# Gate matrices by three bf16 products per token in place of one fp32 product

## What is computed

```
def peer_ffn(x, wq, keys, U, V):
    ...
    top_s, top_j = lax.top_k(cand, K)
    e1 = jnp.take_along_axis(i1, top_j // K, axis=-1)
    e2 = jnp.take_along_axis(i2, top_j % K, axis=-1)
    idx = e1 * N_KEYS + e2
    gate = jax.nn.softmax(top_s, axis=-1).astype(x.dtype)
    ...
        act = jax.nn.gelu(jnp.einsum('tkd,td->tk', U[it], xt), approximate=False) * gt
        return jnp.einsum('tk,tkd->td', act, V[it])
```

## Time and profile before

| what | value |
|---|---|
| median of 3 runs | 3653.57 us (3648.0 to 3656.35) |
| profiled execution, time | 3648.24 us |
| its span, first to last instruction | 3646.4 us |
| mean granted PE clock | 0.963 |
| PE busy / DVE / ACT | 94% / 54% / 33% of the span |
| chain that ended last | PE 87% of the span, of it L501 42%, L743 30%, L657 7%, L699 5% |

### The profile page before, as it was taken

The page is one execution under the profiler, slowest core; times in us unless marked ns, Lnnn a source line. Parts: engine busy times, 40 slices in busy tenths (PEclk is TensorE's granted clock), DMA queues, the critical chain, the costliest instruction groups (busy, mean ns, idle before and its releaser), DMA issues.

```text
span 3646.4 us, 47438 instructions
## 1 busy us (share of the span) xinstructions
PE 3426.9 (94%) x19384; PEld 2917.3 (80%) x19384; DVE 1979.2 (54%) x3330; ACT 1191.8 (33%) x1795; POOL 20.0 (1%) x41
## 2 busy tenths in 40 slices
PE   8899897999999999999999999798468999999998
PEld 7465546888888888888888888688458999999998
DVE  2204633488855555634444444333935998856665
ACT  1111224322233333333333333424314444444443
POOL 0000000000000000000000000000000000000000
PEclk9889898999999999999999999899789999999999
DMA  5241012355555556576556655222014777788885
GB/s 175 70 128 46 1 41 95 114 168 162 166 166 199 193 182 203 173 246 201 192 190 193 193 190 161 69 83 91 0 58 157 211 212 243 246 275 265 266 260 168
DMA packets 232862, 587.87 MB, mean 161 GB/s; under 512 B 21239, under 2 KB 104264, under 8 KB 229000
## 3 DMA queue, kind: packets, MB, share of 16 engines
q1 hardware_dynamic: 227536, 528.57, 46.2%
q0 software_dynamic: 4208, 53.27, 3.8%
q10 hardware_dynamic: 904, 3.01, 0.2%
HBM read 483.06 MB, written 101.71 MB: 160 GB/s over the span
## 4 chain that ended last, share of the span: by engine, by line
PE 87%; DVE 10%; ACT 2%; issue 1%; DMA 1%; ACTq 0%; SPq 0%; DVEq 0%
PE ps L501 42%; PE ps L743 30%; PE ps L657 7%; PE ps L699 5%; DVE w_lo L1459 1%; PE ps L556 1%; DVE arena L1376 1%; PE ps L618 1%; PE ps L679 1%; DVE arena L1370 1%; PE ps L807 0%; PE ps L626 0%; ACT a_t L890 0%; DVE arena L1611 0%; DVE arena L1378 0%
## 5 line engine op out<-in xcount | busy, mean ns | idle before, releaser
L1459 DVE TENSOR_TENSOR w_lo<-wring,w_hi 128x1024 fp32r<-128x1024 f32 x512 | 626.0, 1223 | 736.5 <-ACT w_hi L1008 735.0
L501 PE MATMUL ps<-a_hi,w_hi 128*128 128x512 f32 (+1 forms) x2048 | 703.6, 344 | 8.5 <-DVE w_lo L1459 4.4
L743 PE MATMUL ps<-act_hi,w_hi 128*128 128x512 f32 (+1 forms) x2048 | 697.6, 341 | 3.4 <-DVE act_lo L1490 3.4
L501 PE MATMUL ps<-a_hi,w_lo 128*128 128x512 f32 (+1 forms) x2048 | 690.5, 337 | 0.0
L501 PE MATMUL ps<-a_lo_q,w_hi 128*128 128x512 f32 (+1 forms) x2048 | 690.0, 337 | 0.0
L743 PE MATMUL ps<-act_lo,w_hi 128*128 128x512 f32 (+1 forms) x2048 | 688.8, 336 | 0.0
L743 PE MATMUL ps<-act_hi,w_lo 128*128 128x512 f32 (+1 forms) x2048 | 688.3, 336 | 0.0
L1008 ACT CAST w_hi<-wring 128x1024 fp32r<-128x1024 f32 x512 | 534.3, 1044 | 226.3 <-PE ps L743 226.2
L501 PEld LDWEIGHTS ps<-a_hi,w_hi 128*128 128x128 f32 x2048 | 390.0, 190 | 48.6 <-DVE w_lo L1459 7.0
L743 PEld LDWEIGHTS ps<-act_hi,w_hi 128*128 128x128 f32 x2048 | 388.5, 190 | 50.1 <-issue 3.6
L501 PEld LDWEIGHTS ps<-a_hi,w_lo 128*128 128x128 f32 x2048 | 389.6, 190 | 42.0
(11 more groups left out here) (226 smaller groups left out, 3597.4 us busy)
## 6 DMA issues: line engine op xcount, KB each, us to landing
wring<-in_u SPq DMA_DIRECT2D x256, 512.0 KB, 4.1
wring<-in_v SPq DMA_DIRECT2D x256, 512.0 KB, 4.1
gates<-arena POOLq DMA_DIRECT2D x24, 2048.0 KB, 7.6
acts<-arena SPq DMA_DIRECT2D x128, 256.0 KB, 4.6
arena<-acts SPq DMA_DIRECT2D x128, 256.0 KB, 3.5
arena<-gates SPq DMA_DIRECT2D x16, 2048.0 KB, 11.4
aring<-in_ada SPq DMA_DIRECT2D x56, 512.0 KB, 5.1
wring<-in_ada SPq DMA_DIRECT2D x40, 512.0 KB, 3.7
```

The source lines that it names most:

```text
L501: ins = pe.matmul(o, l, r, start=n == 0, stop=n == len(pairs) - 1, **kw)
L743: ins = pe.matmul(value_sum(l, c), w, x, start=m == 0 and n == 0 and (l == 0 or c % 2 == 0), stop=m == NKEY - 1 and n == 2, skip_group_che ...
L1459: tt(WLO[:, k % 4].rearrange("p k n -> p (k n)"), wring[:, n % RING * TILE:(n % RING + 1) * TILE], WHI[:, k % 4].rearrange("p k n -> p (k ...
```

## The change

Both one-hots become bf16, and the gate is split in three bf16 parts, high, middle and rest, whose sum is the fp32 gate. Each token's product is made of three bf16 products into the same PSUM range, with the same stationary one-hot and one part each of the moving side. All one-hots have keys outside and tokens inside, as EQK had, so the operands of the matmuls are read with a step of 8 bf16 elements. The buffers move within the arena; KEYNUM, which holds the key numbers in that layout, now serves e2 also.

```
+        OHB = over("second_onehot", 22528, 2 * P * OCT, BF16)[:, :].rearrange("p (b e u) -> p b e u", b=2, u=OCT)
+        OHA = over("gated_onehot", 23552, 6 * NKEY * OCT, BF16)[:, :].rearrange("p (b x e u) -> p b x e u", b=2, x=3,
+                                                                               u=OCT)
...
                     for u in range(4):
-                        ins = pe.matmul(ps[:, 2 + h, u * NKEY:(u + 1) * NKEY], OHB[:, n % 2, 4 * h + u, :],
-                                        OHA[:, n % 2, 4 * h + u, :], start=True, stop=True)
+                        for x in range(3):
+                            ins = pe.matmul(ps[:, 2 + h, u * NKEY:(u + 1) * NKEY], OHB[:, n % 2, :, 4 * h + u],
+                                            OHA[:, n % 2, x, :, 4 * h + u], start=x == 0, stop=x == 2)
...
-                    step.done(dve.tensor_copy(KEY1[:, i * P:(i + 1) * P], SL[:, 1, i * P:(i + 1) * P]))
+                    t = slice(i * P, (i + 1) * P)
+                    dve.tensor_copy(KEY1[:, t], SL[:, 1, t])
+                    dve.tensor_copy(KEY2[:, t], SL[:, 2, t])
+
+                    step.done(dve.tensor_copy(GHI[:, t], SL[:, 0, t]))
+                    step.done(tt(GREST, SL[:, 0, t], GHI[:, t], ALU.subtract))
+                    step.done(dve.tensor_copy(GMID[:, t], GREST))
+                    step.done(tt(GLO[:, t], GREST, GMID[:, t], ALU.subtract))
                 toks = slice(n * OCT, (n + 1) * OCT)
-                shape = [P, OCT, NKEY]
-                tt(EQK[:, n % 2], KEYNUM, KEY1[:, toks].unsqueeze(1).to_broadcast([P, NKEY, OCT]), ALU.is_equal)\
-                    .then_inc(S["eq_ready"], 1)
+
+                def spread(x):
+                    return x[:, toks].unsqueeze(1).to_broadcast([P, NKEY, OCT])
+
+                tt(EQK[:, n % 2], KEYNUM, spread(KEY1), ALU.is_equal).then_inc(S["eq_ready"], 1)
                 wait(dve, S["oh_used"], 2 * (o - 1))
-                tt(OHB[:, n % 2], iota[:, :].unsqueeze(1).to_broadcast(shape),
-                   SL[:, 2, toks].unsqueeze(2).to_broadcast(shape), ALU.is_equal)
+                tt(OHB[:, n % 2], KEYNUM, spread(KEY2), ALU.is_equal)
                 yield
                 dve.wait_ge(S["eq_ready"], o + 1)
-                tt(OHA[:, n % 2], EQK[:, n % 2].rearrange("p e u -> p u e"),
-                   SL[:, 0, toks].unsqueeze(2).to_broadcast(shape), ALU.mult).then_inc(S["oh_ready"], 1)
+                for x, part in enumerate((GHI, GMID, GLO)):
+                    ins = tt(OHA[:, n % 2, x], EQK[:, n % 2], spread(part), ALU.mult)
+                ins.then_inc(S["oh_ready"], 1)
```

More of the change, by code:

```diff
@@ L270, in build @@
                     for n, at in (("w_hi", 14336), ("w_lo", 18432))]
-        OHB = view(22528, "p (b u e) -> p b u e", b=2, u=OCT, e=P)
-        OHA = view(24576, "p (b u e) -> p b u e", b=2, u=OCT, e=NKEY)
         ACH, ACL = [over(n, at, ZRING * T)[:, :].rearrange("p (r t) -> p r t", r=ZRING)
@@ L278, in build @@
         KEYNUM = over("key_numbers", 33792, P * OCT, BF16)[:, :].rearrange("p (e u) -> p e u", u=OCT)
+        OHB = over("second_onehot", 22528, 2 * P * OCT, BF16)[:, :].rearrange("p (b e u) -> p b e u", b=2, u=OCT)
+        OHA = over("gated_onehot", 23552, 6 * NKEY * OCT, BF16)[:, :].rearrange("p (b x e u) -> p b x e u", b=2, x=3,
+                                                                               u=OCT)
         KEY1 = over("slot_keys", 34304, T, BF16)[:, :]
+        KEY2, GHI, GMID, GLO = [over(n, at, T, BF16)[:, :] for n, at in
+                                (("slot_keys2", 12288), ("gate_hi", 12544), ("gate_mid", 12800), ("gate_lo", 13056))]
+        GREST = arena[:, 13312:13312 + P]
         I16 = iota[:, 0:TOPK]
```

## The result

The change makes the kernel slower: 4266.57 us median (4262.81 to 4267.28) against 3654.96 us, a ratio of 1.1675 (95% interval 1.1655 to 1.1695). That is above the stated range. The profiled execution took 4262.81 us, with a span of 4261.0 us against 3646.4 and a mean granted clock of 0.889 against 0.963.

The account below looks back on a forecast made before the run. PE's gate-turn work was taken to bound the kernel. 3648.24 us plus 86 us for slower gate products gave 3734 us, or 3740 us as median, with DVE costed at nothing; range 3614 to 3990 us, some 0.12 outside.

Parts of the forecast that it names:

- What bounds the kernel: In both layers' gate turns PE alone sets the pace; its time on an oct is on the path, 96 x 1.79 us.
- The break-even of 0.0746 us a matmul: PE's gate products: 24 bf16 matmuls replace an oct's 16 records of 1.79 us, gaining only if each costs less.
- The low end: Gate matmuls at full column rate, weight load hidden: 0.058 to 0.066 us each, 37 to 18 us back; chance 0.33.
- The step of 16 bytes: PE's gate-matmul reads: the step halves the column rate, 0.112 us a matmul, 0.89 us more an oct; chance 0.34.
- the one by ratio: DVE's stepped read, 1.7 times as slow per element, carried to PE's gate matmuls: about 0.097 to 0.105 us each.
- the way by time: DVE's stepped read of 1.8 ns an element, carried to PE's gate matmuls: 0.23 us for 128 columns.
- The term of 86 us: PE's gate products over 96 octs: 2.68 us an oct, 0.89 us more than now.
- the second rival: PE's gate matmuls pay a whole line's time per column: 331 to 370 us more, about 3985 to 4020 us; chance 0.22.
- what would make me wrong altogether: In the gate turns, PE beginning to wait for DVE, or PE's granted clock falling from 1.00; no size given.
- DVE's part: One-hot work per oct: four bf16 operations of 0.687 us, 2.75 us against 3.23, hidden behind PE and costed at nothing.
- The Trainium skill's rule on lines: SBUF reads: 16-byte lines, two hits a line for full bandwidth, new lines pay; yet 8 bf16 is a free step.
- The third rival: Something else per gate matmul sets the pace, 0.072 to 0.097 us: 12 us more in all; chance 0.11.

## Why the prediction was wrong

- **What bounds the kernel** held. PE has no idle time in the gate turns, and what an oct costs PE is on the path one for one: the blocks of the change account for 370 us, and those of dense fp32 products for 343 of 341.
- **The break-even of 0.0746 us a matmul** held: 0.058 us gave a gain, 0.119 a loss.
- **The low end**, 0.058 to 0.066 us with the weight load hidden, is what a bf16 matmul costs without the large step: 0.057 us with both flat, 0.058 with a step of 4 bytes, 0.064 with flat columns and weights at 16 bytes.
- **The step of 16 bytes: the mechanism was right and its size wrong.** This is the first step that failed. L1446 was the right row to read. I had two ways to carry it over and chose a value near the one by ratio, 0.112 us a matmul; it measured 0.235, near the way by time. The term of 86 us was 370, the top of the second rival, which I had given 0.22. Of the 0.235 us, 0.008 are the weights' step; the moving side alone takes (0.227 - 0.005) / 128 = 1.73 ns a line. That lies between the two rows that I had: 1.8 ns an element in L1446, 1.67 ns for 16 bytes in the fp32r stream. The runs don't tell which of the two it goes with, nor why VectorE and TensorE come so close. What I held against that rival, that PE knows its addresses ahead, spared it nothing.
- **The clock: a missing term.** This is the second. Every case was worked out at a granted clock of 1.00; I named its fall as what would make me wrong altogether and gave it no price and no reason for none. It costs 242 us here. The second rival by its own sum is 4020 us at most; the rest of the way to 4266 is the clock. No row of before foretold the fall: the clock is 1.00 there even beside the late products, 2 columns wide. They don't bring it down by themselves; behind slow blocks it falls.
- **The range** was too narrow for its own chances. It ended at 3990 us, while the second rival, with 0.22, reached from 3985 to 4020; so more than the 0.12 that I named lay outside. With all of that rival inside, the measured time would still have been above it.
- **DVE's part** held: 0.69 us for each bf16 operation, and it waits longer for PE (639.8 us in layer 0, 199.4 before).
- **The Trainium skill's rule on lines** ("SBUF — State Buffer", the note on cachelines in the section on the DMA port swizzle). The runs agree that a line is 16 bytes and that a step to a new line each time costs: the price doubles from 4 to 8 to 16 bytes and stays at 32. They disagree that 8 bf16 are a free step: that is the full price, 0.235 us against 0.058. Two hits in a line, which the rule calls enough, still cost PE 0.119 us; only four (4 bytes) were free here.
- **The third rival** fell. The 81 ns of the Trainium skill ("TensorE: Matmul & The Clock Gate", section "Back-to-back issue gap") are not seen: the stream of weight load and matmul ran at 0.058 us.

Open: what exactly the clock follows. The runs show that it falls in both layers with blocks of slow columns of 5.45 us and more; that with blocks of 1.90 to 3.63 us it falls only in the turns with late products; that the same slow matmuls one by one between fp32r ones leave it at 1.00 in layer 1; and that dense blocks of 1.79 and 5.36 us leave it there too.

## What to carry to other kernels

Look at the step in bytes of the moving operand of every matmul, and compare the rate at which it needs new 16-byte lines with what a stepped read elsewhere in the same trace shows in ns. Here that number, carried over as a time, came close (1.8 ns against 1.73), and as a share of the rate it did not; one case doesn't make that a rule, so let the range hold both. Two tokens inside served both engines here: VectorE kept its fast rate (0.69 us) and TensorE its own (0.058 us). Where a change slows a matmul stream, price the clock as well: neighbours that are not touched can run at half clock behind it, above all behind a long slow block or where other thin matmuls stand next to it.

## What the runs showed that I had not expected

- TensorE's moving side takes a 16-byte line every 1.7 to 1.8 ns, whatever it uses of it: 0.058, 0.119, 0.235 and 0.239 us for 128 bf16 columns with a step of 4, 8, 16 and 32 bytes, with the weights stepped too; 0.227 us at 16 bytes with flat weights, and 0.227 us for a record of 128 fp32 columns with a step of 16 bytes.
- TensorE went to half clock while busy without a gap, and its slow blocks took the same at a clock of 1.00 (5.64 us) as with the clock at 0.84 (5.63). Busy time in the profile says nothing of it; the granted clock and the matmuls' durations (0.39 and 0.63 us for the same 512 columns) do.
- Weight loads mind the step less: their records last 0.147 us at 16 bytes against 0.097 at 4, and a step of 16 bytes costs 0.007 to 0.008 us a matmul (0.064 against 0.057 us, 0.235 against 0.227).
- The 24 fp32r products behind a fast bf16 block cost 0.07 us more than behind an fp32 one (5.53 us in place of 5.46). It is not the type alone: behind the bf16 blocks with a step of 8 bytes they take 5.45 us.
